# Latent pages by gathers of two slots, rotary products as 64x64 tiles over two chunks, and a new spreading of the key gathers in a decoder step

## What is computed

```python
def mla_attend(q_lat, q_pe, q_pos, c_kv, k_pe, w_uv):
    s = jnp.einsum('bqhc,bkc->bhqk', q_lat, c_kv) + jnp.einsum('bqhr,bkr->bhqk', q_pe, k_pe)
    s = s.astype(jnp.float32) * MLA_SCALE
    s = jnp.where(k_pos[None, None, None, :] <= q_pos[None, None, :, None], s, NEG_INF)
    p = jax.nn.softmax(s, axis=-1).astype(c_kv.dtype)
    o_lat = jnp.einsum('bhqk,bkc->bqhc', p, c_kv)
    ...
# sample_layer: 8 sequences, 8 new tokens each, 4096 past tokens in 32 pages of 128
ckv_all = jnp.concatenate([paged_rows(pool_ckv).astype(c_kv.dtype), c_kv], axis=1)
kpe_all = jnp.concatenate([paged_rows(pool_kpe).astype(k_pe.dtype), k_pe], axis=1)
mla_o = mla_attend(q_lat, q_pe, pos, ckv_all, kpe_all, lw['w_uv'])
idx = indexer_topk(q_i, w_i, pos, ik_all, topk)            # 256 keys per query
k_sel = gather_selected(pool_k.astype(k_b.dtype), page_table, k_b, idx, past_len)
v_sel = gather_selected(pool_v.astype(v_b.dtype), page_table, v_b, idx, past_len)
dsa_o = dsa_attend(q_b, pos, k_sel, v_sel, idx)
```

## Time and profile before

| | us |
|---|---|
| median of three runs (lowest, highest) | 1749.44 (1742.18, 1750.18) |
| the profiled execution, its own time | 1741.32 |
| its span, first to last instruction | 1739.5 |
| PE busy in the span | 1626.2 |
| DVE, ACT, POOL busy | 866.3, 421.6, 337.0 |

### The profile page before, as it was taken

The page is one execution under the profiler, slowest core; times in us unless marked ns, Lnnn a source line. Parts: engine busy times, 40 slices in busy tenths (PEclk is TensorE's granted clock), DMA queues, the critical chain, the costliest instruction groups (busy, mean ns, idle before and its releaser), DMA issues.

```text
span 1739.5 us, 21664 instructions
## 1 busy us (share of the span) xinstructions
PE 1626.2 (93%) x8572; PEld 999.0 (57%) x8572; DVE 866.3 (50%) x1636; ACT 421.6 (24%) x1111; POOL 337.0 (19%) x348
## 2 busy tenths in 40 slices
PE   6999989999999898998687899999999999989998
PEld 3554444446776666665454566547777777744443
DVE  3448798998522887874877742222322323210011
ACT  2131312001015545644355531001111111100010
POOL 2000000010004777770555630000000000000000
PEclk9899989999999999998798899999999999999999
DMA  8311212142306788877555845302122122111100
...
DMA packets 89846, 218.38 MB, mean 126 GB/s; under 512 B 13576, under 2 KB 37520, under 8 KB 83696
## 3 DMA queue, kind: packets, MB, share of 16 engines
...
HBM read 199.99 MB, written 16.84 MB: 125 GB/s over the span
## 4 chain that ended last, share of the span: by engine, by line
PE 77%; DVE 9%; POOL 6%; issue 3%; DMA 3%; ACT 2%; ACTq 0%; SPq 0%; DVEq 0%
PE PS L630 13%; PE PS L2063 13%; PE PS L2108 11%; PE PS L2091 7%; PE PS L681 7%; POOL mem L1820 5%; PE PS L2040 4%; PE PS L1538 2%; PE PS L746 2%; PE PS L2017 2%; DVE mem L1732 2%; PE PS L1408 2%; DVE mem L1731 1%; PE PS L1051 1%; PE PS L2471 1%
## 5 line engine op out<-in xcount | busy, mean ns | idle before, releaser
L630 PE MATMUL PS<-mem 128*128 128x512 f32 (+3 forms) x580 | 234.8, 561 | 0.0
L2063 PE MATMUL PS<-mem 128*128 128x376 f32 x704 | 231.7, 481 | 0.0
L2108 PE MATMUL PS<-mem 128*128 128x512 f32 (+1 forms) x440 | 192.2, 599 | 1.4 <-DVE mem L2287 1.4
L2063 PEld LDWEIGHTS PS<-mem 128*128 128x128 f32 x704 | 131.0, 189 | 79.3
L630 PEld LDWEIGHTS PS<-mem 128*128 128x128 f32 (+1 forms) x580 | 100.5, 186 | 119.8 <-issue 119.5
L1820 POOL DMA_INDIRECT mem<-in_cache_dsa_k,mem x128 | 143.9, 1124 | 43.6 <-issue 38.4
L1820 POOL DMA_INDIRECT mem<-in_cache_dsa_v,mem x128 | 122.5, 957 | 145.4 <-PE PS L1520 113.1
L2108 PEld LDWEIGHTS PS<-mem 128*128 128x128 f32 (+1 forms) x440 | 80.7, 184 | 112.3 <-issue 110.7
L2091 PE MATMUL PS<-mem 128*128 128x216 f32 x704 | 135.8, 345 | 0.0
L2091 PEld LDWEIGHTS PS<-mem 128*128 128x128 f32 x704 | 129.2, 189 | 10.7
L2268 DVE TENSOR_SCALAR mem<-mem 128x528 f32<-128x528 f32 x22 | 12.2, 555 | 238.8 <-ACT mem L2171 238.8
...
## 6 DMA issues: line engine op xcount, KB each, us to landing
...
```

What stands on the lines that cost most here:

```text
L630: ins = pe.matmul(PS[0:n, b[bank], out_at:out_at + width], left[:, k, cols], w[:, k, at:at + width], start=k == 0, stop=k == k_range - 1)
L2063: pe.matmul(PS[:, 3 * (f % 2) + j, 0:UP_A], w[:, k, :], h2T[:, k, 0:UP_A], start=k == 0, stop=k == KD - 1)
L2108: return pe.matmul(PS[0:TW[m], (5 * n + m) % 8, :], upT[:, f, token_cols(m)], w[:, i, :], start=f == 0, stop=f == NF - 1)
```

## The change

- A latent gather brings two slots, 2 MB: 16 of them instead of 32, into four pairs of slots. Two pairs are loaded in phase A, where three slots were. A pair is gathered anew when both its chunks are used.
- For each pair of chunks the rotary products come together, as 64x64 tiles (64 rows contract, in two halves LO and HI that work on different chunks): one phase between the two f of the odd chunk, the second behind it, with a wait for the first (rotary_half).
- The own-token products of all batches are made in batch 0, and DVE copies its part per batch.
- The previous batch's outputs stand behind chunk 1 (AHEAD 2). ACT makes exp before the copies of chunk 2. PE waits for ACT's scores where it had waited for DVE's new_scored. DVE scores key rows in two bursts per batch, from batch 0 on (K_FROM 1).
- Turned probabilities lie where the V heads (vb) were, and one of the score rows in another region. The reloads are SP's, and vb's waits for the last outputs.
- The stage no longer waits for the stored gates on PE, ACT and DVE; POOL waits for them before latent gather 2, SP at its start.
- In phase A two heads' keys are made by one matmul of 128 output partitions (4 kn units instead of 8). The turns of x tiles 2 to 4 stand behind unit 1 instead of unit 0.

```diff
-        slots = [C2.take(2048) for _ in range(4)]
-        slots[3:3] = [mem[:, vb_at:vb_at + 2048]]
-        slots += [C.take(2048) for _ in range(3)]
+        slot_pairs = [r.take(4096) for r in (C2, C2, C, C)]
...
-        row_scores = [C.take(ROW) for _ in range(2)]
+        row_scores = [C.take(ROW), C3.take(ROW)]
...
-        probsT = C3.take(17, 128)
+        probsT = mem[:, vb_at:vb_at + 2048].rearrange("p (j r) -> p j r", j=16)
+        probsT_new = C3.take(128)
...
-        units += [("wt", 0)] + [("kn", h) for h in range(H)] + [("kl", 0), ("ql", 0), ("ql", 1)]
+        units += [("wt", 0)] + [("kn", p) for p in range(H // 2)] + [("kl", 0), ("ql", 0), ("ql", 1)]
...
-                    ins = pe.matmul(PS[0:64, b[0], :], wuk[:, c, 64 * m:64 * m + 64], ckvT[:, c, 0:512],
+                    ins = pe.matmul(PS[:, b[0], :], wuk[:, c, 128 * m:128 * m + 128], ckvT[:, c, 0:512],
...
-                for h in range(H):
+                for p in range(H // 2):
                     for c in range(2):
-                        ins = pe.matmul(PS[0:64, b[0], 16 * h:16 * h + 16], wuk[:, c, 64 * h:64 * h + 64],
+                        ins = pe.matmul(PS[:, b[0], 16 * p:16 * p + 16], wuk[:, c, 128 * p:128 * p + 128],
...
-        AHEAD = 3
+        AHEAD = 2
         ROWS_B = 0
-        K_FROM = 4
+        K_FROM = 1
...
+        def gates_done(eng):
+
+            for i in range(2):
+                eng.wait_ge(sem(f"gates_stored{i}"), upto(f"gates_stored{i}", len(gate_tiles) - 2 + i))
+
...
-            if n >= 8:
-                gp.wait_ge(sem("latents_used"), upto("latents_used", n - 8))
-            gp.indirect_dma_start(raw_slot(n), None, ckv_rows,
+            if n >= 4:
+                gp.wait_ge(sem("latents_used"), upto("latents_used", 2 * (n - 4) + 1))
+            gp.indirect_dma_start(slot_pairs[n % 4], None, ckv_rows,
                                   bass.IndirectOffsetOnAxis(ap=idx_ckv[:, b, j:j + 1], axis=0)).then_inc(
-                sem(f"ckv_in{n % 8}"), tick(f"ckv_in{n % 8}", n, by=16))
+                sem(f"ckv_in{n % 4}"), tick(f"ckv_in{n % 4}", n, by=16))
...
+            sp.wait_ge(sem("latents_used"), upto("latents_used", 4 * (NB - 2) + 3))
+            sp.dma_start(flat(qT)[0:96], scratch["qT"]).then_inc(sem("heads_back"), tick("heads_back", by=16))
+            sp.wait_ge(sem("latent_dots"), upto("latent_dots", NB - 1, 3))
+            sp.dma_start(mem[:, lent_end:qb_at], scratch["qi"]).then_inc(sem("qi_back"), tick("qi_back", by=16))
+            sp.dma_start(flat(kT)[0:96], scratch["kT"]).then_inc(sem("heads_back"), tick("heads_back", by=16))
+            sp.dma_start(flat(vm)[:, 0:2048], scratch["vm"][:, 0:2048]).then_inc(
+                sem("heads_back"), tick("heads_back", by=16))
+            sp.dma_start(flat(vm)[0:16, 2048:2560], scratch["vm"][0:16, 2048:2560]).then_inc(
+                sem("heads_back"), tick("heads_back", by=16))
+            sp.wait_ge(sem("latents_used"), upto("latents_used", 4 * (NB - 1) + 3))
+            sp.dma_start(vb[:, 0:4, :], O["new_v_p"][0, 0, 0:512].rearrange("(m p) h d -> p m (h d)", p=128)
+                         ).then_inc(sem("vb_back"), tick("vb_back", by=16))
...
-            phase_a_done(pe)
+            pe.wait_ge(sem("turned_act"), upto("turned_act", "kb", 4, 0))
...
+                    if b == 0 and k == 0:
+                        wait_unit_read(pe, ("gt", len(gate_tiles) - 1))
                     if k >= 2:
                         pe.wait_ge(sem("scored"), upto("scored", b, k - 2))
                     elif b:
-                        pe.wait_ge(sem("new_scored"), upto("new_scored", b - 1)) if k == 0 else pe.wait_ge(sem("scored"), upto("scored", b - 1, 3))
+                        pe.wait_ge(sem("scored"), upto("scored", b - 1, k + 2))
                     pe.wait_ge(sem("sturn_out"), upto("sturn_out", ("c", b, k, 1, 1)))
-                    half = [PS[64 * u:64 * u + 64, k % 2, :] for u in range(2)]
                     for f in range(2):
                         for u in range(2):
-                            ins = pe.matmul(half[u], q2[f], latT(("c", b, k, u, f)), start=f == 0, stop=False,
-                                            skip_group_check=True)
+                            ins = pe.matmul(PS[64 * u:64 * u + 64, k % 2, :], q2[f], latT(("c", b, k, u, f)), start=f == 0,
+                                            stop=False, skip_group_check=True)
+                        if k % 2 and f == 0:
+                            if k == 1:
+                                pe.wait_ge(sem("sturn_out"), upto("sturn_out", ("p", b, 1)))
+                                pe.wait_ge(sem("qpe_spread"), upto("qpe_spread", b))
+                            rotary(b, k, 0).then_inc(sem("rotary_half"), tick("rotary_half", b, k))
...
-                    if k == 0:
-                        pe.wait_ge(sem("sturn_out"), upto("sturn_out", ("p", b, 1)))
-                        pe.wait_ge(sem("qpe_spread"), upto("qpe_spread", b))
-                    for q in range(4):
-                        for u in range(2):
-                            ins = pe.matmul(half[u][:, 128 * q:128 * q + 128], qpe_z[:, b % 2, q, :],
-                                            kpeT[b % 2][:, 2 * k + u, :], start=False, stop=q == 3,
-                                            skip_group_check=True)
-                    ins.then_inc(sem("latent_dots"), tick("latent_dots", b, k))
+                    if k % 2:
+                        pe.wait_ge(sem("rotary_half"), upto("rotary_half", b, k))
+                        rotary(b, k, 1).then_inc(sem("latent_dots"), tick("latent_dots", b, k))
+                        same(("latent_dots", b, k - 1), ("latent_dots", b, k))
+                    if k == 0 and b == 0:
+                        new_tokens()
                     if k == AHEAD - 1 and b:
                         outputs(b - 1)
...
-                pe.wait_ge(sem("scored"), upto("scored", b, 2))
-                new = slice(NT * b, NT * b + NT)
-                for f in range(2):
-                    pe.matmul(PS[0:64, 0, 0:NT], q2[f], ckv_new[:, f, new], start=f == 0, stop=False)
-                pe.matmul(PS[0:64, 0, 0:NT], qpe_s[0:32, 64 * b:64 * b + 64],
-                                 kpe_new[0:32, NT * b:NT * b + NT], start=False, stop=True).then_inc(
-                    sem("latent_dots"), tick("latent_dots", b, 4))
+
+            def rotary(b, k, phase):
+
+                for q in range(2):
+                    for u in range(2):
+                        for half, r in enumerate((LO, HI)):
+                            c, i = k - 1 + (half + phase) % 2, 2 * half + q
+                            ins = pe.matmul(PS[64 * u:64 * u + 64, c % 2, 128 * i:128 * i + 128], qpe_z[r, b % 2, i, :],
+                                            kpeT[b % 2][r, 2 * c + u, :], start=False, stop=phase == 1,
+                                            skip_group_check=True)
+                return ins
+
+            def new_tokens():
+
+                for b in range(NB):
+                    new, q = slice(NT * b, NT * b + NT), slice(64 * b, 64 * b + 64)
+                    out = PS[0:64, 3, 64 + NT * b:64 + NT * b + NT]
+                    for f in range(2):
+                        pe.matmul(out, ql_s[:, f, q], ckv_new[:, f, new], start=f == 0, stop=False)
+                    ins = pe.matmul(out, qpe_s[0:32, q], kpe_new[0:32, new], start=False, stop=True)
+                ins.then_inc(sem("own_dots"), tick("own_dots"))
...
+            wait_stored(act, "vb")
+            act.wait_ge(sem("stored_vb_s"), upto("stored_vb_s", 4))
...
-                for k in range(4):
-                    if k < 3:
-                        turn_out(b, k + 1)
-                    if k == 0 and b >= 2:
-                        turn_rows(b - 2)
-                    act.wait_ge(sem("latent_dots"), upto("latent_dots", b, k))
-                    act.mul(row_scores[b % 2][:, 512 * k:512 * k + 512], PS[:, k % 2, :], MLA_SCALE).then_inc(
-                        sem("scored"), tick("scored", b, k))
+                turn_out(b, 1)
+                if b >= 2:
+                    turn_rows(b - 2)
+                if b == ROWS_B:
+                    act_sturn(act, ("n", b), row_no, PS[:, sturn_bank(("n", b)), 0:128]
+                              .rearrange("p (a n) -> p a n", a=2))
+                if b:
+                    exp(b - 1)
+                for k in (0, 2):
+                    turn_out(b, 2 + k // 2)
+                    for c in (k, k + 1):
+                        act.wait_ge(sem("latent_dots"), upto("latent_dots", b, c))
+                        act.mul(row_scores[b % 2][:, 512 * c:512 * c + 512], PS[:, c % 2, :], MLA_SCALE).then_inc(
+                            sem("scored"), tick("scored", b, c))
                     if k == 0 and b:
-                        exp(b - 1)
-                    if k == 1 and b + 1 < NB:
+                        outputs(b - 1)
```

(47 more changed lines are left out.)

50 lines of the change are left out of this document (23 added, 27 removed).

## The result

The changed kernel took 1733.90 us as the median of 11 runs (1732.16 to 1744.21), the kernel before 1748.22 as the median of its 11 (1741.01 to 1750.21): a ratio of 0.994, with a 95% interval from 0.9919 to 0.9962. That is 14 us by the medians, 10 by the ratio. The forecast of 1720 meant 29 against the 1749.44 that it started from: the time lies inside the range, the gain is a third to a half of what was said. Both kernels' runs fall into two groups, 7 to 8 us apart (1732 to 1734 and 1740 to 1744 now, 1741 to 1743 and 1748 to 1750 before); the lower one holds 7 of 11 runs now and 4 of 11 before, so that the two medians lie in different groups, while group by group the means differ by 8.8 and 7.8 us. The two profiled executions, 1732.90 and 1741.32, are both of the lower group, so their traces can be set side by side: 8.4 us.

A forecast was written before the change was run, and what follows sets the result against it. POOL's issue rate was taken as the bound between 600 and 757 us, PE close behind. Stage -17 and phase A -7.9 made -25 us: 1716 against the profiled run, 1724 against the median, forecast 1720, range 1704 to 1741.

The forecast's parts named there:

- POOL ceased to bound: Latent stage: POOL's period per batch falls from 32.2 to 27.3 us, below PE's 28.9.
- the rival of late latents: Latent stage: 2 MB gathers land late, each batch waits 3.5 to 4 us; 1738 us, chance 0.19.
- The rotary products in fours: PE, latent stage: 64x64 tiles run four at once, gaining 0.4 us per pair, 0.8 per batch.
- the 0.15 that the prediction read: PE, latent stage: a seam with a change of tile form costs about 0.15 us, one without 0.05.
- 6.9 forecast for kn alone: Phase A, L657: 8 full-width products remain of 16 at 0.86 us each, -6.9 us.
- -1.0: Phase A, L662: its 32 records in 1.98 us lose half, -1.0 us.
- I follow it: row 10 scored at 577.5: Latent stage's head: row 10 scored at 577.5, batch 2 gathered at 582, first dots at 596.5, 1.6 us later.
- about +4 once, at the stage's start, where batch 2's latents set the time of what follows: PE, batch 0: all own-token products move there, -0.5 us per batch against about +4 once.
- I add 0.9 us per batch, a period of 29.8: Latent stage: the wait for latents' landing nearly touches, adding 0.9 us to PE's period of 28.9.
- Rival 4: Latent stage: DVE's bursts of key rows hold up ACT's exponentials; +27 us, 1776 as a median, chance 0.05.
- The x turns: Phase A: turns of x tiles 2 to 4 move behind unit 1, counted at nothing.
- The tail: Batch 7: own dots about -2.3 us, ACT's reloads gone -0.7.

The follow-up runs named there:

- e4: Changed kernel with both chunks' rotary products in one go behind the odd chunk's dots, 128 rows contracting, no 64x64 tiles; 1740.82 us.
- e7: Kernel before, with only the prompt's keys of two heads made by one product; 1737.15 us against 1746.66.
- e1: Changed kernel with ACT's spreading of the next batch's rotary queries moved to behind the previous batch's turned probabilities; 1731.93 us.
- f1: Changed kernel with earlier spreading, earlier division, x turns behind unit 0, and sparse row 11's products made five times; 1723.62 us.
- g1: As f1 but without the repeated products of sparse row 11, on the chip of its partner run with them; 1728.80 us.
- g3: Changed kernel with sparse row 11's products in the prompt's stage made five times over; 1731.35 us.
- e2: Changed kernel with K_FROM 4 as before, so key rows are spread from batch 0's end on; 1743.03 us.
- e6: Changed kernel leaving out the product of every second gathered key row with its query on DVE (wrong scores); 1733.50 us.
- e5: Changed kernel with e1's edit and DVE's division of the previous batch behind the second burst's first key row; 1732.79 us.
- e3: Changed kernel with the turns of x tiles 2 to 4 behind unit 0 again; 1730.66 us.

## Why the prediction was wrong in size

**Right.** POOL ceased to bound (its gaps show it), a gather of 16 KB per partition issues like one of 8, and the rival of late latents did not come: 9.8 us of landing where 11.3 were assumed, so the 0.9 us for it were not needed. The rotary products in fours gave what was taken, 0.4 us per pair: dots and rotary products of a pair cost 2 x 2.75 = 5.50 us from start to start in the earlier trace rows and 1.87 + 3.22 = 5.09 now (against the form of e4 the gain is 0.31). The Trainium skill (TensorEngine Tiling (Array Packing), Key Properties) says that a change of tiling mode drains TensorE. The trace agrees in direction: 0.60 us for a phase whose two steps of 0.22 are 0.44, so 0.16 for the seam, the 0.15 that the prediction read. The kn products, with kl's, gave 7.0 us in e7, all of them kept, against 6.9 forecast for kn alone. The other part of that term did not come: the kl products stayed at 1.8 us to the next start with half as many (1.85 against 1.98 in the records), so -1.0 was wrong.

**Wrong, head of the stage: 8 us.** The first dots of batch 2 were put 6.3 us before has them and came 1.8 after. The step that failed is "I follow it: row 10 scored at 577.5": it opens DVE's burst when the scores are there and lets the rows run, with the landing of their keys put at nothing. Shifted by the 7.9 us that it took off phase A, its burst opens at 540.1, row 2 follows at 542.7 and row 10 is scored at 569.6. In the trace row 2's keys landed only at 548.34, 12.87 us after their gather. Row 2 started 5.7 us late, 1.8 of which are phase A's, and row 10 was scored at 575.3, 5.7 late; so between them the rows ran as worked out. Behind it POOL took 0.6 us more to the latents' gather, these 0.7 more to land, and their turns, at a clock of 0.50 to begin with, 1.0. The trace of before already had such a landing, in front of its own first key row:

```profile
542.25 12.69 DMA mem<-in_cache_dsa_k,mem
```

The own-token products are the obvious suspect ("about +4 once, at the stage's start, where batch 2's latents set the time of what follows"). They lie in the way of the scores, and row 1 did start at 544.49, 4.4 us behind the working. But that path ended 1.4 us before the landing, so in this trace they cost nothing. Other traces agree: row 1 starts 286.5 us behind the kn products in some and 288 in others (e1, f1, g1, g3), row 2 at 289.8 to 291.1 in all variants but e2, and at 290.5 to 290.9 in those four. In e6, where DVE was through with row 1 sooner, row 2 started no sooner. In e1, e4 and g3 DVE did not wait for row 2's keys, so the two paths end within some 2 us of each other, and to start batch 2 sooner both would have to be shorter. That is read from chains and starts; no run moved the own-token products, or row 2's gather ahead of batch 1's latents.

**Wrong, the body: 6.6 us of 15.7.** The five periods took 155.6 us, not 149. PE's own work was 29.3 where 28.9 was forecast. The second step that failed is "I add 0.9 us per batch, a period of 29.8": in the trace PE waited for latents in no batch from 3 on, and a wait that the sum doesn't have stood in its place. The missing term was ACT: moving the spreading behind the last pair of scores, and the pair's scores together, put 1.5 us more work between PE's last rotary product and the first copy it waits for. The prediction followed every wait of PE, POOL and DVE, and for ACT only the exponentials. Rival 4, which had DVE's bursts hold up ACT, had the right cause and the wrong victim: it looked at the maximum for exp, with 5 us of slack, and not at the division that stands behind the same burst. Of the 6.6 us the three periods with 1.16 us of waiting hold 2.1, the two with a late division 4.5. e1 and e5 settle it: without either wait the periods are 29.6 to 29.9.

**Wrong, at nothing: 2 to 3 us.** The x turns were counted 0, within 2 us; e3 gives 2.2. In the two traces of the table they are 1.4 of the 1.8 us by which phase A ended late.

**The tail** gave 1.7 us instead of 3, and behind the mark 0.7 were lost; no run tells why. Together, against the profiled run: -25 predicted, 8.0 + 6.6 + 1.3 + 0.7 lost, -8.4 in the trace. The forecast of 1720 laid 4 us more on top, half of the step to the median of three runs, and some 6 of the 14 us between the two medians are the swing's: that by the medians half of the forecast gain is there is in part luck.
